# Where a 576-column product is cut: 288 and 288, or 320 and 256 over two PSUM banks

## The reference, cut to what matters

```python
x = x + 0.5 * swiglu(rmsnorm(x, g_ffa[i]), w_ffa_in[i], w_ffa_out[i])   # 1024 -> 2 x 2816 -> 1024
h = rmsnorm(x, g_mix[i])
x = x + mix                          # layer 0: latent attention; layer 1: chunkwise mLSTM
x = x + 0.5 * swiglu(rmsnorm(x, g_ffb[i]), w_ffb_in[i], w_ffb_out[i])
gate = jax.nn.sigmoid(rmsnorm(x, g_ple[i]) @ w_ple_gate[i])
x = x + gate * (ps[g][i] @ w_ple_proj[i])
```

## Time and profile before

| what | value |
|---|---|
| time, median of 2 runs | 2850.88 us (2850.66 to 2851.09) |
| the profiled execution: span from first to last instruction | 2847.9 us |
| what lies around the span, against that median | 3.0 us |
| PE busy, weight loads busy | 96%, 91% |
| DVE, ACT, POOL busy | 51%, 24%, 31% |
| mean granted TensorE clock | 0.970 |

### The profile page before, as it was taken

One profiled execution on the slowest core, in us unless ns is written; L12 is line 12 of the kernel. 1 busy time (PEld: TensorE's weight loads), 2 busy tenths in 40 slices (PEclk: granted clock), 3 DMA queues, 4 the chain that ended last, 5 costly groups with the idle time before them and its releaser, 6 DMA issues.

```text
span 2847.9 us, 49206 instructions
## 1 busy us (share of the span) xinstructions
PE 2746.0 (96%) x19103; PEld 2578.7 (91%) x19103; DVE 1448.7 (51%) x1615; ACT 674.3 (24%) x984; POOL 882.8 (31%) x424
## 2 busy tenths in 40 slices
PE   7999999899999899999998999999999999999998
PEld 7999999666666799999998999999987799999998
DVE  5555325666443475553256555324533475554236
ACT  3222112344332122221123222112121122222122
POOL 2333333000010233333333333333320043333332
PEclk9999999999999999999999999999996799999999
DMA  4222222212332122222222222223321122222222
GB/s 131 81 81 82 74 83 67 55 22 55 83 80 76 30 82 81 81 79 76 81 83 82 83 85 80 71 81 94 81 59 63 43 80 83 85 83 69 82 82 74
DMA packets 423789, 215.45 MB, mean 76 GB/s; under 512 B 54933, under 2 KB 420890, under 8 KB 423706
## 3 DMA queue, kind: packets, MB, share of 16 engines
q1 hardware_dynamic: 421206, 210.88, 25.9%
q10 hardware_dynamic: 2500, 3.50, 0.4%
HBM read 206.57 MB, written 7.76 MB: 75 GB/s over the span
## 4 chain that ended last, share of the span: by engine, by line
PE 90%; DVE 7%; issue 2%; ACT 0%; DMA 0%; ACTq 0%; DVEq 0%; POOL 0%
PE ps L1688 25%; PE ps L1690 25%; PE ps L1693 25%; PE ps L689 2%; PE ps L721 2%; PE ps L672 1%; PE ps L656 1%; DVE S L544 1%; PE ps L1190 1%; DVE PP L473 1%; PE ps L707 1%; PE ps L1205 1%; DVE st L466 1%; PE ps L1225 1%; PE ps L1216 1%
## 5 line engine op out<-in xcount | busy, mean ns | idle before, releaser
L1350 POOL TENSOR_TENSOR wlo<-raw,whi 128x1024 fp32r<-128x1024 f32 (+3 forms) x383 | 831.4, 2171 | 1473.1 <-ACT whi L1388 1473.1
L1688 PE MATMUL ps<-xh,whi 128*128 128x288 f32 x3568 | 770.3, 297 | 11.0 <-DVE xl L1515 7.3
L1690 PE MATMUL ps<-xl,whi 128*128 128x288 f32 x3568 | 768.3, 297 | 0.0
L1693 PE MATMUL ps<-xh,wlo 128*128 128x288 f32 x3568 | 768.0, 297 | 0.0
L1388 ACT ACTIVATE whi<-raw 128x1024 fp32r<-128x1024 f32 (+3 forms) x383 | 368.3, 962 | 1493.8 <-PE ps L1693 1482.0
L1688 PEld LDWEIGHTS ps<-xh,whi 128*128 128x128 f32 x3568 | 572.5, 189 | 12.8 <-issue 5.8
L1693 PEld LDWEIGHTS ps<-xh,wlo 128*128 128x128 f32 x3568 | 573.4, 189 | 0.0
L1690 PEld LDWEIGHTS ps<-xl,whi 128*128 128x128 f32 x3568 | 573.0, 189 | 0.0
L1688 PE MATMUL ps<-uh,whi 128*128 128x288 f32 x1408 | 302.7, 296 | 0.0
L1693 PE MATMUL ps<-uh,wlo 128*128 128x288 f32 x1408 | 302.7, 296 | 0.0
L1690 PE MATMUL ps<-ul,whi 128*128 128x288 f32 x1408 | 302.7, 296 | 0.0
(11 more groups left out here) (336 smaller groups left out, 2605.9 us busy)
## 6 DMA issues: line engine op xcount, KB each, us to landing
raw<-in_w_ffa_in SPq DMA_DIRECT2D x88, 512.0 KB
raw<-in_w_ffb_in SPq DMA_DIRECT2D x88, 512.0 KB
pages<-in_cache_ckv SPq DMA_DIRECT2D x128, 128.0 KB, 2.0
raw<-in_w_ffa_out SPq DMA_DIRECT2D x32, 384.0 KB
raw<-in_w_ffb_out SPq DMA_DIRECT2D x32, 384.0 KB
raw<-in_w_mlstm_in SPq DMA_DIRECT2D x24, 512.0 KB
raw<-in_w_ffa_out SPq DMA_DIRECT2D x32, 320.0 KB
raw<-in_w_ffb_out SPq DMA_DIRECT2D x32, 320.0 KB
```

Source lines behind the costliest of these rows:

```text
L1350: pool.tensor_tensor(lo[:, 0:n, :], raw[:, p % RAW, 0:n, :], hi[:, 0:n, :].bitcast(F32), ALU.subtract).then_inc(wlo_ready, 1)
L1688: mm(out[:, q, :], hi[:, n, :], h0[:, q, :], start=first and n == 0, stop=False)
L1690: mm(out[:, q, :], hi[:, n, :], l0[:, q, :], start=False, stop=False)
L1693: ins = mm(out[:, q, :], lo[:, n, :], h0[:, q, :], start=False, stop=end)
```

## The change

Tokens are cut at 320 in place of 288. A tile takes columns 192 to 511 of the first bank and 0 to 255 of the second, which is one run of 576 columns in the flattened pair of banks, so every reader takes it as a plain run and `half` goes. The number and order of matmuls, weight loads, waits, DMAs and reads stay as they were.

```diff
-H = T // 2
+TA = 320
+SPANS = (slice(0, TA), slice(TA, T))
...
-        def half(t):
-            return t.rearrange("p (h n) -> p h n", h=2)
-
         def slot(t):
-            return ps[:, 2 * (t % 2):2 * (t % 2) + 2, 0:H]
+            b = 2 * (t % 2)
+            return ps[:, b:b + 2, :].rearrange("p b n -> p (b n)")[:, 512 - TA:512 - TA + T]
...
-                    act.activation(Q[0:64, 0, :].rearrange("p (h n) -> p h n", h=2), ps[0:64, 0:2, 0:H], ACT.Copy).then_inc(qn_taken, 1)
+                    act.activation(Q[0:64, 0, :], slot(0)[0:64, :], ACT.Copy).then_inc(qn_taken, 1)
...
-                        dve.tensor_tensor(half(tA[:, :]), slot(ta), half(r[:, :]), ALU.mult).then_inc(tile_taken, 1)
+                        dve.tensor_tensor(tA[:, :], slot(ta), r[:, :], ALU.mult).then_inc(tile_taken, 1)
...
-                    h0, l0 = half(mh(n)), half(ml(n))
-                    for q in (0, 1):
-                        mm(out[:, q, :], hi[:, n, :], h0[:, q, :], start=first and n == 0, stop=False)
-                    for q in (0, 1):
-                        mm(out[:, q, :], hi[:, n, :], l0[:, q, :], start=False, stop=False)
+                    xh_n, xl_n = mh(n), ml(n)
+                    for t in SPANS:
+                        mm(out[:, t], hi[:, n, :], xh_n[:, t], start=first and n == 0, stop=False)
+                    for t in SPANS:
+                        mm(out[:, t], hi[:, n, :], xl_n[:, t], start=False, stop=False)
                     end = last and n == n_chunks - 1
-                    for q in (0, 1):
-                        ins = mm(out[:, q, :], lo[:, n, :], h0[:, q, :], start=False, stop=end)
+                    for t in SPANS:
+                        ins = mm(out[:, t], lo[:, n, :], xh_n[:, t], start=False, stop=end)
```

More of the change, by code:

```diff
@@ L338, in mla_acts @@
                     act.wait_ge(panel_used, PH + h + 2 + d4)
-                    act.activation(Q[0:64, 1, :].rearrange("p (h n) -> p h n", h=2), ps[0:64, 0:2, 0:H], ACT.Copy).then_inc(qn_taken, 1)
+                    act.activation(Q[0:64, 1, :], slot(0)[0:64, :], ACT.Copy).then_inc(qn_taken, 1)
                     for hh in (0, 1):
@@ L402, in mla_dves @@
                 dve.wait_ge(panel_used, PM + k + 1)
-                dve.tensor_tensor(half(zc[:, k, :]), slot(t0 + k), half(r[:, :]), ALU.mult).then_inc(tile_taken, 1)
+                dve.tensor_tensor(zc[:, k, :], slot(t0 + k), r[:, :], ALU.mult).then_inc(tile_taken, 1)
                 dve.wait_ge(tile_taken, t0 + k + 1)
@@ L442, in rope_query @@
                 dve.wait_ge(panel_used, PH + h + 1 + dh)
[L443 to L444 removed]
+                link(dve.tensor_tensor(qtmp[64:96, :], slot(0)[96:128, :], rope[96:128, :], ALU.mult))
+                link(dve.tensor_tensor(Q[64:96, hh, :], slot(0)[64:96, :], rope[64:96, :], ALU.mult))
                 dve.tensor_tensor(Q[64:96, hh, :], Q[64:96, hh, :], qtmp[64:96, :], ALU.add).then_inc(qr_taken, 1)
@@ L601, in query @@
                     def query(hh):
-                        products(PH + h + hh, d4, 3, lambda n: cqh[:, n, :], lambda n: cql[:, n, :], ps[:, 0:2, 0:H])
+                        products(PH + h + hh, d4, 3, lambda n: cqh[:, n, :], lambda n: cql[:, n, :], slot(0))
                     query(0)
@@ L945, in mlstm_dves @@
             dve.wait_ge(panel_used, GP + 1)
-            tg = 2 * (GT % 2)
-            link(dve.tensor_tensor(half(RA[0:LH, :]), ps[0:LH, tg:tg + 2, 0:H], half(r[0:LH, :]), ALU.mult))
-            dve.tensor_tensor(half(RB[0:LH, :]), ps[32:32 + LH, tg:tg + 2, 0:H], half(r[32:32 + LH, :]), ALU.mult).then_inc(tile_taken, 1)
+            link(dve.tensor_tensor(RA[0:LH, :], slot(GT)[0:LH, :], r[0:LH, :], ALU.mult))
+            dve.tensor_tensor(RB[0:LH, :], slot(GT)[32:32 + LH, :], r[32:32 + LH, :], ALU.mult).then_inc(tile_taken, 1)
             dve.wait_ge(tile_taken, GT + 1)
@@ L969, in evacuate @@
                 if t < 4:
-                    dve.scalar_tensor_tensor(out=half(dst), in0=slot(IT + t), scalar=DK ** -0.5, in1=half(r[:, :]),
+                    dve.scalar_tensor_tensor(out=dst, in0=slot(IT + t), scalar=DK ** -0.5, in1=r[:, :],
                                              op0=ALU.mult, op1=ALU.mult).then_inc(tile_taken, 1)
                 else:
-                    dve.tensor_tensor(half(dst), slot(IT + t), half(r[:, :]), ALU.mult).then_inc(tile_taken, 1)
+                    dve.tensor_tensor(dst, slot(IT + t), r[:, :], ALU.mult).then_inc(tile_taken, 1)
             L = slice(0, LH)
@@ L1556, in ffn_in @@
                         dve.wait_ge(chain, cl + 1 + i * 4)
-                        dve.tensor_tensor(half(ub[:, :]), slot(ta + 1), half(sA[:, :]), ALU.mult).then_inc(tile_taken, 1)
+                        dve.tensor_tensor(ub[:, :], slot(ta + 1), sA[:, :], ALU.mult).then_inc(tile_taken, 1)
                         dve.wait_ge(tile_taken, ta + 2 + i * 4)
@@ L1570, in update @@
                 def update(xf, t):
-                    dve.scalar_tensor_tensor(out=half(xf), in0=slot(t), scalar=0.5, in1=half(xf),
+                    dve.scalar_tensor_tensor(out=xf, in0=slot(t), scalar=0.5, in1=xf,
                                              op0=ALU.mult, op1=ALU.add).then_inc(tile_taken, 1)
@@ L1580, in update @@
                 def update(xf, t):
-                    dve.tensor_tensor(half(xf), slot(t), half(xf), ALU.add).then_inc(tile_taken, 1)
+                    dve.tensor_tensor(xf, slot(t), xf, ALU.add).then_inc(tile_taken, 1)
                 chunks(T0[name], nxt, ready, update)
@@ L1592, in gate @@
                     gc = sg[:, bass.ds(c, 1), :].rearrange("p a t -> p (a t)")
-                    dve.tensor_tensor(half(gc), slot(t), half(r[:, :]), ALU.mult).then_inc(tile_taken, 1)
+                    dve.tensor_tensor(gc, slot(t), r[:, :], ALU.mult).then_inc(tile_taken, 1)
                 def proj(c, k, kdyn, p, t, dyn, cl, cdyn):
@@ L1599, in proj @@
                     xf = x[:, bass.ds(c, 1), :].rearrange("p a t -> p (a t)")
-                    dve.tensor_tensor(half(ub[:, :]), slot(t), half(gc), ALU.mult).then_inc(chain, 1)
+                    dve.tensor_tensor(ub[:, :], slot(t), gc, ALU.mult).then_inc(chain, 1)
                     dve.wait_ge(chain, cl + 1 + cdyn)
```

## The result

| | before | after |
|---|---|---|
| time, median of 2 runs | 2850.88 us (2850.66 to 2851.09) | 2821.53 us (2817.46 to 2825.61) |
| profiled execution: span | 2847.9 us | 2823.8 us |
| mean granted TensorE clock in it | 0.970 | 0.966 |

The ratio is 0.9894, 95% interval [0.9857, 0.993]: 1.1% faster, less than the 2% that the prediction called a difference, and inside its range of 2820 to 2890 us by 1.5 us. But no change was forecast, and the interval leaves out 1. So the case is one of a small gain whose source the prediction did not see.

The account below looks back on a forecast made before the run. PE was taken to bind, three quarters of the time in split matmuls of 288 columns. Every part of the change was put at about nothing: 2847.9 + 0 us span plus 3.0 us around it, 2851 us, range 2820 to 2890.

Parts of the forecast that it names:

- Bound by PE, 8,088 pairs, 266.7 ns each: Split products on PE: 8,088 pairs of 288-column matmuls at 266.7 ns a pair, 75.7% of the span.
- Any straight line a + bN gives 2a + 576b, the same for both cuts: Pairs of split matmuls: cost linear in columns, so 320 + 256 take 266.7 ns like 288 + 288, change 0.
- The half-clock row: Split matmuls at 1.2 GHz: 240.0 ns each, exactly 288 columns, taken as support for the straight line.
- The plain float32 rows: Plain float32 matmuls: 379, 486 and 594 ns at 256, 384 and 512 columns, taken as lying on a straight line.
- Bounds of the pair, 244 to 281 ns: A 320 + 256 pair was to cost -22 to +15 ns against now, -180 to +120 us over 8,088 pairs.
- any pair under 262 or over 271 ns would make the forecast wrong: Sign to check in the timeline after: time of a 320 + 256 pair, forecast at 267 ns.
- What the rows leave open: Means of one matmul's large forms differ, 296 to 299 ns, unexplained; as much on a pair would be 24 us either way.
- Weight loads under 256 columns: A 111 ns load fits under a 256-column matmul of 118 to 120 ns, 7 to 9 ns left; nothing late.
- Contiguous tiles, 0 to -13 ns beside PE: DVE's reads of a tile as one run: 0 to -13 ns each, from 758 ns, beside PE's next tile.
- Whole blocks of 64: Rival: columns rounded up to multiples of 64, so a pair costs 244 ns, -180 us, 2671 us; chance 0.11.
- The weight floor: Rival: 256 columns stay at 133.3 ns, 320 pay 146.7 to 148.1; +108 to +120 us, about 2965 us; chance 0.09.
- The third, both matmuls under one loop: Rival: 320 and 256 columns both cost 133.3 ns, pair 266.7, 2851 us; counted with the forecast's 0.80.

Follow-up runs that it names:

- `widths`: Kernel before with each long stage given its own pair of mostly equal widths, 224 to 384: 117.4 ns a matmul at 256 columns, 146.7 at 320.
- `cut316`: Kernel after with the cut at 316 and 260 columns in place of 320 and 256: 2806.85 us, ratio 0.9848.
- `cut312`: Kernel after with the cut at 312 and 264 columns in place of 320 and 256: 2811.98 us, ratio 0.9855.
- the padded kernels: 96 bytes of padding put ahead of the activation tiles, in after (2815.12 us, run again 2823.35 us) and in before (2819.99 us).
- `cut352`: Kernel after with the cut at 352 and 224 columns in place of 320 and 256: 2908.58 us, ratio 1.0199.
- `run288`: Kernel after, contiguous tiles kept, with the cut put back to 288 and 288 columns: 2850.94 us, ratio 0.9999.
- `before_pad64`: Kernel before, cut at 288, with 64 bytes of padding ahead of the activation tiles: 2851.83 us, one run.

## Why the prediction was wrong, step by step

**Bound by PE, 8,088 pairs, 266.7 ns each: held.** 344 chunks at 13.3 ns less give 4.59 us, and such a stage gained 4.58. The long stages together gained 30.0 us; 4.0 us at the lower clock in `ple` and a start 1.4 us later took from it, and the span got 24.1 us shorter.

**"Any straight line a + bN gives 2a + 576b, the same for both cuts", "I take the straight line, change 0": this step failed.** The mechanism named was right in one point, that the 13.3 ns come on top of the columns and vanish at 1.2 GHz, and `widths` shows that they are a fixed amount for equal widths from 288 up. What was wrong is that this amount belongs to the matmul. It belongs to the running chunk, which can have 780, 787, 793 or 800 ns at the same 576 columns a pair. The term was set to 0 and measures -4.4 ns a pair (800 to 786.7 ns for three), which is 36 us over 8,088 pairs if all ran at full clock; 30.0 us of it came in the long stages. The half-clock row was called "exact columns" and taken as support for the line; it could not be, since what matters vanishes there, as the prediction itself had said. The plain float32 rows were the other support. They are durations, not distances of starts, and 107 ns for 128 columns is the pace of 1.2 GHz, so they too say nothing of what comes on top of the columns at 2.4. What makes the pace of a chunk stays open.

The Trainium skill, in "TensorE: Matmul & The Clock Gate" under "Back-to-back issue gap", has N / 2.4 + 2.5 ns at full clock as the gap of single matmuls without the loads between them; an estimate by that is 735 ns for six. No run of a chunk of 1,728 columns here comes near: the best is 780, in `cut316`, `cut312` and the padded kernels.

**Bounds of the pair, 244 to 281 ns: held** (262), and so, by a hair, did the line "any pair under 262 or over 271 ns would make the forecast wrong": it was too wide a gate for the question whether there is a gain at all. The same list's 752 matmuls in 100 us, pairs of 267 ns and starts of 147 and 120 ns failed: 765, 262, and 146 and 117.

**"What the rows leave open", 3 ns either way, 24 us: about the right size, by luck.** The 3 ns in the means of the earlier trace rows are not the term that moved: a chunk took 800 ns in every long stage of before, and the median duration of a matmul of line 1688 at full clock is 296 or 297 ns in every stage. The 299 is also no large form's, but that of the smallest, with 64 matmuls. So the lower end of the range, 2820 us, holds the measured time thanks to an allowance for something else.

**Weight loads under 256 columns: held.** 256 columns take 116.7 to 117.9 ns in these runs and a load 111 to 112; at 224 the load ends last, +13.3 ns over the 260 that 576 columns can have. The Trainium skill, in the same page under "LDWEIGHTS", gives a load of 128 columns P / 1.2 = 107 ns; by an estimate from it, 256 columns at 2.4 GHz (107 ns) are the narrowest that cover a load. At full clock `widths` agrees to 5 ns, with 111.5 ns at 224 columns, where the load ends last. At the lower clock the loads of `cut352` and of line 1216 take 213.3 ns, twice that figure and again the time of 256 columns.

**Contiguous tiles, 0 to -13 ns beside PE: held**, at 0: DVE's read takes 758 ns, and `run288` is 0.9999 of before.

**The rivals fell.** Whole blocks of 64: 320 columns cost 145.6 ns and not 133.3, and 304 cost less than 320 (140.0 against 146.7 in `widths`). The weight floor: 256 columns go well under 133 ns. The third, both matmuls under one loop, would show 133 and 133; the starts are 146 and 117.

## What to carry to other kernels

If a matrix engine is bound by a repeated chunk, measure the time of the chunk from start to start and compare it with its bare columns: here 800 against 720 ns, and 20 of the 80 could be had by moving the cut by 28 columns, with no other work. The price of this loop was a property of its pattern and addresses, not a sum of prices per instruction, so try a few neighbouring cuts and a few paddings of the operand on the chip; and take one that is fast in every execution (316 + 260 here, five runs within 1 us), since others may be as fast in one run and not in the next. Stop where the narrow part no longer covers a weight load.

## What the runs showed that was not expected

- **The pace of a chunk comes in steps.** In the kernels' own order six matmuls of 576 columns a pair took, in the mean, 780.0, 786.7, 793.3 or 800.0 ns (790.0 where 787 and 793 take turns), 6.7 ns apart, the time of 16 columns at 2.4 GHz. 352 + 224 took 820.0. In before and after single distances within a chunk vary (113 to 147 ns in after) while the chunk repeats to the nanosecond; in others (`cut316`, `before_pad64`) chunks of a few ns more and less alternate.
- **It depends on where the rows lie.** Equal widths: 800 ns with rows 160 or 224 bytes past a multiple of 256, 793.3 at 192, 780 (with one stage at 800) at 0. 32 and 64 bytes of padding have one run each.
- **It can depend on how a series of chunks begins.** With 320 + 256 or 288 + 288 on padded rows, and with 312 + 264, a series that nothing interrupts has 780 or 800 ns and holds it; for padded 320 + 256, which one differed between two executions of one kernel. Unpadded 256 + 320 had 790.0 in some series and 786.7 in others. Unpadded 288 + 288, 320 + 256 and 316 + 260 had one pace in all long stages of the executions profiled.
- **What sets the steps is open.** Not the order of the six, not PSUM's layout, not DVE's reads; those were tried, and a smaller load gave no gain at 288. Whether the cut works through the widths or through the byte at which the second part begins was not separated: no run has 288 + 288 with a second part at a multiple of 256 past the first. That weight loads and streaming columns get in each other's way on reading SBUF would fit, and no run shows it. Where the weights lie was not varied; the padding changed the distance from them to the rows together with the rows' place.
